# Weight sums of a seven-product projection stored and loaded unsplit, and split again in each span

## The reference, cut to what matters

```python
h2 = _rmsnorm(x, g_ffn) * (1 + sc2) + sh2
g = h2 @ f_w_gate                     # 1024 x 2816
u = h2 @ f_w_up                       # 1024 x 2816
gconv, new_fconv = _causal_dwconv(g, f_conv, f_conv_w, f_conv_b)   # 3 taps
x = x + gt2 * ((jax.nn.silu(gconv) * u) @ f_w_down)
# after the layer: y = _rmsnorm(x, g_final)
```

## Time and profile before

| what | value |
|---|---|
| runs, us | 2828.19, 2833.49, 2839.77 (median 2833.49) |
| profiled execution, us | 2836.62, its span 2834.9 |
| PE busy, share of the span | 2684.7 us, 95% |
| DVE, ACT busy | 53%, 40% |
| HBM read, written | 390.88 MB, 140.75 MB |
| mean granted TensorE clock | 0.974 |

### The profile page before, as it was taken

The page is one execution under the profiler, slowest core; times in us unless marked ns, Lnnn a source line. Parts: engine busy times, 40 slices in busy tenths (PEclk is TensorE's granted clock), DMA queues, the critical chain, the costliest instruction groups (busy, mean ns, idle before and its releaser), DMA issues.

```text
span 2834.9 us, 42942 instructions
## 1 busy us (share of the span) xinstructions
PE 2684.7 (95%) x15479; PEld 2375.0 (84%) x15479; DVE 1490.0 (53%) x2851; ACT 1129.7 (40%) x1949; POOL 258.2 (9%) x412
## 2 busy tenths in 40 slices
PE   4999999999777999999799999999999999999998
PEld 2888888999755777777699997789999888999987
DVE  3533334323236666665777776645444564655546
ACT  2333324323332454544544444433333443444444
POOL 0100000000023333432000000000000000000000
PEclk8999999999867999999899999999999999999999
DMA  9443434212365434442777775748777575787756
GB/s 325 138 151 115 148 99 152 95 66 75 108 205 180 148 126 139 136 130 89 240 264 240 239 254 183 268 156 271 229 224 225 198 257 182 260 273 262 250 188 211
DMA packets 355271, 531.44 MB, mean 187 GB/s; under 512 B 28084, under 2 KB 253510, under 8 KB 354930
## 3 DMA queue, kind: packets, MB, share of 16 engines
q1 hardware_dynamic: 348836, 522.61, 55.5%
q10 hardware_dynamic: 6288, 6.88, 0.8%
HBM read 390.88 MB, written 140.75 MB: 188 GB/s over the span
## 4 chain that ended last, share of the span: by engine, by line
PE 44%; DMA 4%; DVE 2%; issue 1%; ACT 1%; SPq 1%; DVEq 0%; POOL 0%; POOLq 0%; ACTq 0%
PE acc_ps L3495 11%; PE acc_ps L3484 10%; PE acc_ps L3483 10%; PE acc_ps L3482 10%; DMA f_raw_g<-in_f_w_down 3%; PE acc_ps L3546 2%; DMA f_w_lo<-scratch_sums 1%; ACT f_w_hi L3705 0%; DVE f_h_lo L3994 0%; DMA scratch_sums<-f_w_lo 0%; DVE f_w_lo L3956 0%; SPq L3304 0%; DMA f_mid_raw<-scratch_mid 0%; DVE f_y L4025 0%; DVE f_w_lo L3961 0%
## 5 line engine op out<-in xcount | busy, mean ns | idle before, releaser
L3482 PE MATMUL acc_ps<-f_h_hi,f_w_hi 128*128 128x384 f32 (+1 forms) x1816 | 592.0, 326 | 16.6 <-PEq L4248 5.9
L3483 PE MATMUL acc_ps<-f_h_lo,f_w_hi 128*128 128x384 f32 (+1 forms) x1816 | 595.8, 328 | 0.0
L3484 PE MATMUL acc_ps<-f_h_hi,f_w_lo 128*128 128x384 f32 (+1 forms) x1816 | 594.4, 327 | 0.0
L3482 PEld LDWEIGHTS acc_ps<-f_h_hi,f_w_hi 128*128 128x128 f32 x1816 | 342.6, 189 | 19.6 <-issue 13.9
L3484 PEld LDWEIGHTS acc_ps<-f_h_hi,f_w_lo 128*128 128x128 f32 x1816 | 343.0, 189 | 0.0
L3483 PEld LDWEIGHTS acc_ps<-f_h_lo,f_w_hi 128*128 128x128 f32 x1816 | 342.0, 188 | 0.1
L959 PE MATMUL p_unit<-w_in_hi,p_ht_hi 128*128 128x512 f32 (+1 forms) x544 | 205.0, 377 | 9.8 <-DVE p_ht_lo L698 7.5
L3956 DVE TENSOR_TENSOR f_w_lo<-f_raw_g,f_w_hi 128x1024 fp32r<-128x1024 f32 x104 | 127.3, 1224 | 162.8 <-PE acc_ps L3495 113.3
L959 PE MATMUL p_unit<-w_in_hi,p_ht_lo 128*128 128x512 f32 (+1 forms) x544 | 200.7, 369 | 0.0
L959 PE MATMUL p_unit<-w_in_lo,p_ht_hi 128*128 128x512 f32 (+1 forms) x544 | 200.3, 368 | 0.0
L1072 PE MATMUL p_unit<-p_ht_hi,w_in_hi 128*128 128x384 f32 (+1 forms) x576 | 190.2, 330 | 2.8 <-DVE p_ht_lo L742 1.5
(11 more groups left out here) (596 smaller groups left out, 4974.3 us busy)
## 6 DMA issues: line engine op xcount, KB each, us to landing
f_raw_g<-in_f_w_down SPq DMA_DIRECT2D x114, 512.0 KB, 3.4
f_w_hi<-scratch_sums SPq DMA_DIRECT2D x84, 512.0 KB, 4.4
f_w_lo<-scratch_sums SPq DMA_DIRECT2D x84, 512.0 KB, 5.6
f_raw_g<-in_f_w_gate SPq DMA_DIRECT2D x64, 512.0 KB, 4.2
scratch_sums<-f_w_hi SPq DMA_DIRECT2D x44, 512.0 KB, 2.7
scratch_sums<-f_w_lo SPq DMA_DIRECT2D x44, 512.0 KB, 3.5
f_mid_raw<-scratch_mid SPq DMA_DIRECT2D x110, 192.0 KB, 3.3
scratch_mid<-f_mids SPq DMA_DIRECT2D x44, 384.0 KB, 2.7
```

Of the source, the lines that this page charges most:

```text
L3482: t.matmul(dst, hi, h_hi[:, op, k, 0:w], start=(opening and k == 0), stop=False, skip_group_check=True)
L3483: t.matmul(dst, hi, h_lo[:, op, k, 0:w], start=False, stop=False, skip_group_check=True)
L3484: last = t.matmul(dst, lo, h_hi[:, op, k, 0:w], start=False, stop=(k == 3), skip_group_check=True)
```

## The change

The sums are stored and loaded as they are formed, unsplit: two transfers of 512 KB for a unit in place of four, both ways.

- Span 0: `store_sums` waits for the sums and no longer for the low halves. `add_weights` waits until the stores of the unit before have landed, since it overwrites `sum`. The waits of ScalarE for the stores of split halves go.
- Spans 1 and 2: `load_sums` loads into `sum` as soon as low 2 (low 3) of the unit before has read it. ScalarE's high 2 and high 3 wait for the loads (`s_sld`) and are done in all spans, at the place that they had in span 0; VectorE's low 2 and low 3 likewise. TensorE waits for `s_lo` in all spans.
- Unit 0 of spans 1 and 2: the sums are loaded into `sum` during the second down pass and split at its end; the tiles `early_2`, `early_3` and what goes with them go. SyncE's unit 0 becomes like the others.

```diff
@@ SyncE
             def store_sums(f):
                 for g in (2, 3):
-                    sp.wait_ge(s_lo[g], f + 1)
-                    for n, w in enumerate((w_hi, w_lo)):
-                        sp.dma_start(sums_at(f, 2 * n + g - 2), group(w, g).bitcast(F32)).then_inc(s_sst[g - 2], 16)
+                    sp.wait_ge(s_sum, f * 4 + 2 * (g - 1))
+                    sp.dma_start(sums_at(f, g - 2), sum_pair(g)).then_inc(s_sst[g - 2], 16)
             def load_sums(s, f):
                 n = f + s * KF
-                for g, free in ((2, P5), (3, P3)):
-                    if isinstance(f, int) and f == 1:
-                        sp.wait_ge(s_sld[g - 2], n * 32 - 32 * KF)
-                        for j in range(2):
-                            sp.wait_ge(s_dused[j], s * NPASS * QF)
+                for g in (2, 3):
+                    if isinstance(f, int) and f == 0:
+                        sp.wait_ge(s_sst[g - 2], 16 * KF)
+                        sp.wait_ge(s_tlo, 8 * s)
                     else:
-                        sp.wait_ge(s_prod, n * NP - NP + free)
-                    for m, w in enumerate((w_hi, w_lo)):
-                        sp.dma_start(group(w, g).bitcast(F32), sums_at(f, 2 * m + g - 2)).then_inc(s_sld[g - 2], 16)
+                        sp.wait_ge(s_lo[g], n)
+                    sp.dma_start(sum_pair(g), sums_at(f, g - 2)).then_inc(s_sld[g - 2], 16)
...
@@ SyncE, second down pass of spans 0 and 1
                             elif f == 3:
-                                sp.wait_ge(s_sst[0], 32 * KF)
-                                load_early_sums(s + 1, 2, 0)
-                            elif f == 4:
-                                load_early_sums(s + 1, 2, 1)
+                                load_sums(s + 1, 0)
                             elif f == 5:
-                                sp.wait_ge(s_sst[1], 32 * KF)
-                                for j in range(2):
-                                    sp.wait_ge(s_mst[j], 16 * QF * (s + 1))
-                                load_early_sums(s + 1, 3, 1)
                                 load_up(s + 1, 0, 1)
-                            elif f == 7:
-                                sp.wait_ge(s_lo[4], KF * (s + 1) + 1)
-                                load_early_sums(s + 1, 3, 0)
@@ TensorE
                         if which == P6:
-                            if s:
-                                pe.wait_ge(s_sld[0], n * 32 + (32 - 32 * KF))
-                            else:
-                                pe.wait_ge(s_lo[2], n + 1)
+                            pe.wait_ge(s_lo[2], n + 1)
                             pe.wait_ge(s_p1, n + 1)
...
@@ ScalarE, high
                     act.wait_ge((s_rg if g == 1 else s_ru)[j], q * 16 + (16 * QF * s + 16))
+                elif s:
+                    act.wait_ge(s_sld[g - 2], n * 16 + (16 - 16 * KF))
                 else:
                     act.wait_ge(s_sum, n * 4 + (2 if g == 2 else 4))
                 if not opening:
                     act.wait_ge(s_prod, n * NP - NP + {1: P2, 2: P5, 3: P3, 4: P4}[g])
-                    if g in (2, 3):
-                        act.wait_ge(s_sst[g - 2], n * 32)
                 elif s and g == 1:
                     act.wait_ge(s_dused_hi[0], s * NPASS * QF)
+                elif s and g == 2:
+                    act.wait_ge(s_dused_hi[1], s * NPASS * QF)
+                elif s and g == 3:
+                    for n_ in range(2):
+                        act.wait_ge(s_dused[n_], s * NPASS * QF)
@@ ScalarE, unit
-                elif s == 0:
+                else:
                     high(s, q + j, 1 - j, 2)
                     high(s, q + j, 1 - j, 3)
-                else:
-                    act.wait_ge(s_prod, n * NP + P3)
@@ VectorE, add_weights
+                if not (isinstance(n, int) and n == 0):
+                    dve.wait_ge(s_sst[which], n * 16)
@@ VectorE, start of a span
             for s in range(NSP):
+                if s:
+                    low(s, 0, 0, 2)
                 for i in before(s, None)[:2]:
                     gated(i)
+                if s:
+                    low(s, 0, 0, 3)
```

More of the change, by code:

```diff
@@ L2933, in feed_forward_tiles @@
         F["raw_g"][j] = sb(f"f_raw_g{j}", [P, D])
[L2934 to L2937, removed]
         F["raw_u"][j] = sb(f"f_raw_u{j}", [P, D])
@@ L2945, in feed_forward_tiles @@
     tile("taps", [P, KF, 4])
-    with ExitStack() as overlaid:
-        early, _ = new_pools(nc, overlaid)
-        F["early_2"] = early("f_early_2", [P, 2 * D], F32R)
     tile("sum", [P, 4, BLK])
@@ L2954, in feed_forward_tiles @@
     tile("ss", [P, 4])
-    with ExitStack() as overlaid:
-        early, _ = new_pools(nc, overlaid)
-        F["early_3_lo"] = early("f_early_3_lo", [P, D], F32R)
     tile("mids", [P, 2 * MAXT])
@@ L3078, in feed_forward @@
         cg = F["cg"]
-        early = {2: (F["early_2"][:, 0:D], F["early_2"][:, D:2 * D]), 3: (F["early_3_hi"][:], F["early_3_lo"][:])}
         ml_raw = [raw_u[b // 2][:, b % 2 * LW:(b % 2 + 1) * LW] for b in range(NB4)]
@@ L3202, in load_raw @@
                 load_up(s, q, j)
-            def load_early_sums(s, g, n):
-                sp.dma_start(early[g][n].bitcast(F32), sums_at(0, 2 * n + g - 2)).then_inc(s_sld[g - 2], 16)
             def sums_at(f, at):
@@ L3210, in sums_at, with sum_pair @@
                 return src[:, at * D:(at + 1) * D]
+            def sum_pair(g):
+                return sums[:, 2 * (g - 2):2 * (g - 1), :].rearrange("p s c -> p (s c)")
             def store_sums(f):
                 for g in (2, 3):
-                    sp.wait_ge(s_lo[g], f + 1)
-                    for n, w in enumerate((w_hi, w_lo)):
-                        sp.dma_start(sums_at(f, 2 * n + g - 2), group(w, g).bitcast(F32)).then_inc(s_sst[g - 2], 16)
+                    sp.wait_ge(s_sum, f * 4 + 2 * (g - 1))
+                    sp.dma_start(sums_at(f, g - 2), sum_pair(g)).then_inc(s_sst[g - 2], 16)
             def load_sums(s, f):
                 n = f + s * KF
-                for g, free in ((2, P5), (3, P3)):
-                    if isinstance(f, int) and f == 1:
-                        sp.wait_ge(s_sld[g - 2], n * 32 - 32 * KF)
-                        for j in range(2):
-                            sp.wait_ge(s_dused[j], s * NPASS * QF)
-                    else:
-                        sp.wait_ge(s_prod, n * NP - NP + free)
-                    for m, w in enumerate((w_hi, w_lo)):
-                        sp.dma_start(group(w, g).bitcast(F32), sums_at(f, 2 * m + g - 2)).then_inc(s_sld[g - 2], 16)
+                for g in (2, 3):
+                    if isinstance(f, int) and f == 0:
+                        sp.wait_ge(s_sst[g - 2], 16 * KF)
+                        sp.wait_ge(s_tlo, 8 * s)
+                    else:
+                        sp.wait_ge(s_lo[g], n)
+                    sp.dma_start(sum_pair(g), sums_at(f, g - 2)).then_inc(s_sld[g - 2], 16)
             def store_mid(s, q, j):
@@ L3298, in load_pair @@
                         sp.wait_ge(s_tlo, 8 * s)
+                    else:
+                        for n_ in range(2):
+                            sp.wait_ge(s_sst[n_], 16 * KF)
                 else:
@@ L3461, in unit @@
                     elif which == P7:
-                        if s:
-                            pe.wait_ge(s_sld[1], n * 32 + (32 - 32 * KF))
-                        else:
-                            pe.wait_ge(s_lo[3], n + 1)
+                        pe.wait_ge(s_lo[3], n + 1)
                         pe.wait_ge(s_u2, n + 1)
@@ L3476, in unit @@
                     w_pair = (w_hi, w_lo)
-                    if early_unit(s, q, j) and 2 <= slot < 6:
-                        at = slot % 2 * BLK
-                        w_pair = early[slot // 2 + 1]
                     for k in range(4):
@@ L3700, in down_high @@
                     act.wait_ge(s_prod, (KF * (s + 1) - 1) * NP + (P2, P5)[j])
-                    if s == 0 and j == 1:
-                        act.wait_ge(s_sst[0], 32 * KF)
                 else:
@@ L3824, in _ @@
                         high(s + 1, 0, 0, 1, True)
+                        high(s + 1, 0, 0, 2, True)
+                        high(s + 1, 0, 0, 3, True)
             squares(NT - 1)
@@ L3854, in low @@
                     dve.wait_ge(s_dused[0], s * NPASS * QF)
+                elif g in (2, 3) and early_unit(s, q, j):
+                    for n_ in range(2):
+                        dve.wait_ge(s_dused[n_], s * NPASS * QF)
                 v.tensor_tensor(group(w_lo, g), raw_group(s, q, g, j), group(w_hi, g), ALU.subtract).then_inc(s_lo[g], 1)
```

9 lines of the change are left out of this document (removed).

## The result

The changed kernel takes 2974.86 us as the median of 6 runs (2971.59 to 2988.84), against 2828.80 us for the kernel before (6 runs, 2828.19 to 2839.77). The ratio is 1.0515, 95% interval 1.0496 to 1.0533: 146 us slower. Predicted were 2950 us and a range of 2895 to 2995. The profiled execution took 2986.62 us, 150.0 more than that of before.

What follows compares the result with a forecast made beforehand. TensorE bounds the kernel before; afterwards a ring of waits through the loads of sums would in spans 1 and 2. Span 1 + 39, span 2 + 80, span 0 - 2 sum to + 117: 2950 us, 8 in 10 between 2895 and 2995.

Steps and rivals of the forecast that it cites:

- The ring from mid to mid: Spans 1 and 2: mid(f) comes 15.8 and 15.9 us after mid(f-1), against TensorE's 14.5 and 12.1; chance 0.78.
- The part of the ring behind the landing: Spans 1 and 2: high 2, low 2, C12, convolution, taps and products to the end of mid.
- The landing: Spans 1 and 2: the first load of sums lands 7.5 us after M, the end of the previous mid.
- single 512 KB load: Span 2, kernel before: load of sums behind gate and up weights, 5.3 us, cited against an estimate of M + 6.0.
- Units 3 to 5: Spans 1 and 2, units with outputs: SyncE's output work delays the loads; 21.4, 19.4 and 19.4 us, together 60 per span.
- the predicted gain: Span 0, unit 1: ScalarE's high(3) comes some 2 us sooner, for 2 us less, between 0 and 4.3.
- span 0 keeps 14.5: Sign of being right: span 0's units stay at 14.5 us, since TensorE stays full there.
- Span changes: Between spans: sums of unit 0 are loaded far ahead and low(2) is ready before P6; cost 0, at worst 2 us each.
- hide nothing: Whole kernel: the bytes saved, half of the sums' traffic, hide nothing that TensorE waits for.
- Rival (b): Waits halve TensorE's clock for some 6 us a unit; span 1 units take 17.5 us, total 2984; chance 0.10.
- (a): Loads are hidden, ring doesn't decide; some 2828 us; chance 0.03 for gain over 0.5%, 0.06 within 0.5% shared with (c).
- (c): Spans 1 and 2: only the added splits cost, loads in time; 2833 us; chance 0.06 within 0.5%, shared with (a).

Runs made afterwards that it cites:

- experiment 1: Changed kernel with SyncE loading the raw sums for unit f+2 in unit f, ahead of the store of mid(f): 2826.70 us, ratio 0.9962 to the kernel before.
- experiment 2: Changed kernel with the sums of f+1 loaded ahead of the weights of f+2, still behind the store of mid(f-1): 2876.23 us, ratio 1.0139 to the kernel before.
- experiment 6: Changed kernel with spans 1 and 2's splits of groups 2 and 3 behind the SiLU (ScalarE) and mid(f) (VectorE): 2931.12 us, ratio 1.0351 to the kernel before.
- experiment 7: Changed kernel, spans 1 and 2: high 2 before P1's copy, high 3 behind SiLU, low 2 before mid(f), low 3 behind: 2865.67 us, ratio 1.0110 to before.
- experiment 8: Changed kernel with sums loaded one unit earlier and the two halves at columns 0 and 2048: 2824.73 us, ratio 0.9976 to the kernel before.
- 5: Changed kernel with scratch rows of 2048 numbers instead of 4096, pairs still at columns 0 and 1024: 2974.35 us, ratio 1.0495 to the kernel before.

## Why the prediction was right, and where it was off

- **The mechanism: right.** The ring from mid to mid through SyncE's loads was opened in experiment 1 (all of the loss gone) and shortened in experiment 2 (the time followed the start of high 2 + 8.3).
- **The part of the ring behind the landing: right.** Predicted 8.3 us from the start of high 2 to the end of mid; measured 8.26 in the turn of span 2 above and 8.29 in one of span 1 (2113.72 to 2122.01).
- **The landing: this term was mis-sized.** Taken: M + 7.5. Measured, as the mean of the 17 steady units: M + 8.7 in span 1 and M + 8.6 in span 2. That is 1.1 to 1.2 us in 34 turns, about 39 us, and accounts for the + 17.5 and + 19 by which spans 1 and 2 exceed their sums. It isn't the issue: the first load goes out at M + 2.1, earlier than the M + 2.4 taken. Nor is it that two loads are now in flight together, for they were before. The "single 512 KB load" of the prediction, issued at 2558.57, had the low half of the same weights right behind it:

```profile
2558.57 0.35 SPq L3230 DMA_DIRECT2D f_w_hi<-scratch_sums  x1
2559.09 0.35 SPq L3230 DMA_DIRECT2D f_w_lo<-scratch_sums  x1
```

What the prediction overlooked is where the pair lies. `sums_at(f, 2 * m + g - 2)` put the two halves loaded together at columns 0 and 2048, `sums_at(f, g - 2)` puts them at 0 and 1024. Experiment 3, the changed kernel with 0 and 2048, has the first load landing at M + 7.7 to 7.8 in the same mean (M + 7.8 and 8.0 on the other chip), and the kernel before has M + 7.8 in span 2. So 0.6 to 1.0 us of the miss go with the neighbouring columns; why they cost this is open. The other 0.2 to 0.5 us are, at least in part, a credit for the earlier issue that did not come: in span 2 the kernel before issues at M + 2.8 and experiment 3 at M + 2.1, and both land at M + 7.8. Why the earlier issue bought nothing is open too.
- **Units 3 to 5: right.** 60 us predicted in each span; 58.8 and 61.4 measured. The landing of M + 11 for the later two (measured 10.8, 10.9 in span 1 and 11.8, 10.7 in span 2) is partly luck: it was picked between 7.5 and 13.0, and the first one's 13.0 became 12.8 and 14.1.
- **Span 0: the predicted gain came, and a loss that was not predicted.** TensorE's wait for the copy of P1 in unit 0 is 2.9 us instead of 4.3, and from TensorE's first matmul of the span to mid(1) it is 43.0 us instead of 45.3 (1373.11 to 1416.14 after, 1371.88 to 1417.20 before). That is 2.3 us less, against 2 predicted; part of it lies before mid(0) and so outside the table's row. From mid(1) to mid(20) the span then lost 3.5 us (280.2 for 276.6). No wait of TensorE accounts for it: 515 matmuls stand where 521 stood, 0.1755 us each for 0.1733, at clock 1.00. So "span 0 keeps 14.5", one of the signs of being right, was not met: 14.7. More on this below.
- **Span changes: an unpredicted gain of 8.5 us.** Cost at 0 "at worst 2 each", they became shorter by 3.7 and 4.8. TensorE's waits there, before in 1722:1912 and 2230:2416, after in 1724:1911:

```profile
PE acc_ps L3495 <- ACT f_w_hi L3716: 3.8, 4, 1.8
...
PE acc_ps L3495 <- ACT f_w_hi L3716: 2.9, 1, 2.9
```

```profile
PE acc_ps L3457 <- ACT f_w_hi L3677: 2.3, 2, 1.8
```

In the second change no such wait is left. So 4.4 of the 8.5 us are waits for down weights. The two that are gone, 1.83 us at 1841 and 2.94 at 2348, stand in the second down pass, and in the 7 us behind each the granted clock of the kernel before was 0.76 and 0.79, which is some 1.5 us of full speed each; the changed kernel has 1.00 over the whole of both changes. That makes about 7.5 of the 8.5 us. Experiment 1 has this gain too (5.0 and 4.6 us), and it is most of what that kernel wins over the one before. It fits that the loads of split halves in these passes, four for the next span's unit 0, are now two; but no run separates this from the other edits there. So "hide nothing", said of the saved bytes, isn't borne out for the down passes. In the total this gain hides about a fifth of the landing's miss.
- **Rival (b), the clock: its premise seen, its effect not.** After the wait of 4.87 us the granted clock stood at 0.50, 1.2 GHz, and 12 matmuls ran in 3 us; after the wait of 1.51 us it stayed at 1.00 and 21 ran. The Trainium skill, "TensorE: Matmul & The Clock Gate", section "What's actually happening", has the throttled state as the default that activity releases, which agrees with the first of these rows. But TensorE isn't on the ring while it waits in every unit, so its slow stretch only makes the next wait shorter: the waits go 4.87, 1.51, 4.96 us in turn, and the 8.3 us behind the landing held. In experiment 6, where TensorE is part of the chain, the clock was 1.00 over span 1 and 0.94 over span 2; what the slow stretches of span 2 cost there was not tested.
- **Rivals (a) and (c): refuted** by the mids of the changed kernel, 17.0 and 16.9 us apart. (c) holds for experiment 1, where the added work costs nothing, and in part for experiment 7.

## What to carry to other kernels

Work that fits into an engine's idle time can still cost 5%, if the instruction that waits for its data stands in front of others in an in-order list: draw the loop from the wait, through what is queued behind it, back to what releases the data, and compare its length with the bottleneck's time for one unit. It is cured at either end, by issuing the load a unit earlier or by moving the waiting instruction to where its result is used; but a place that is too late makes another ring, so check it against the first user. Price a moved transfer by a row in which it has the same transfers around it and lies at the same places in HBM. Here the edit moved the halves that are loaded together next to each other, and on one chip this was some 25 of 145 us.

## What the runs showed of the hardware

- Two 512 KB loads issued together right behind the gate and up weights, of columns next to each other (0 and 1024 of the same rows), landed after a median of 6.7 to 6.8 us; of columns 0 and 2048, after 6.1 to 6.2; with the distance between rows halved, 6.7. Issued 2.4 to 2.7 us apart, with the up weights some 4 to 6 us ahead, they took 4.5 (neighbours, experiment 1) and 4.4 (apart, experiment 8). Why neighbours in flight together land later is open.
- The start-to-start time of TensorE's matmuls of 384 columns in span 0, with no wait and full clock, was 0.1733 us in the kernel before and in experiments 1, 2, 3 (both times) and 6, and 0.1755 in the changed kernel (both times), 5, 7 and 8. The gaps repeat: 174, 172, 169, 176, 175, 174 ns in the kernel before, 179, 173, 175 in the changed kernel. The two programs profiled twice gave the same value both times, and neither the columns (experiment 8 has them apart, 1 has not) nor the place of the splits goes with it. It is worth 3.5 us from mid(1) to mid(20) of span 0; its cause is open. Experiment 7 has it in span 1 too (515 in 90 us); experiments 1, 2 and 8, which keep TensorE full there too, have 521 or 522.
